# The first piece of x is issued from ScalarE's DMA queue instead of SyncE's

## The chip, the cores and the metric

The kernel runs on one core of a Trainium2 chip. The metric is device time in microseconds (us), the median over several executions of the whole program. Lower is better.

## The reference, cut to what matters

One layer of a decoder with three parallel branches over 1024 prompt tokens and 32 sample tokens (1056 rows in all, model width 1024):

```
h    = rmsnorm(x) * norm_g
proj = h @ w_in                       # (1056, 1024) x (1024, 4608)
qa, ka, va, ga, xb, gb, qc, kc, vc, gc = split(proj)
oa = rmsnorm(retention(qa, ka, va))   # branch A, 4 heads
ob = rglru(conv4(xb))                 # branch B, width 512
oc = window_attention(qc, kc, vc)     # branch C, window 128, 4 heads, 2 kv heads
y  = x + concat(oa*silu(ga), ob*silu(gb), oc*silu(gc)) @ w_out
```

All data are float32. The outputs are y for both token groups and the new states and caches. The change touches only how the first part of x reaches the chip's memory; nothing of the computation differs.

## The kernel before, in words

Each engine's instructions are written out by hand, one program per engine, and the programs meet at semaphores. There is no scheduler: the order in the file is the order on the engine.

The input projection is cut into 18 weight units of 256 columns. Every product is made in three passes of float32r matmuls (`three_pass`, L408 to L410): operands are split into a high part and a low part. The high part of a weight piece is a ScalarE copy (`w_hi`, L826), its low part a VectorE subtraction (`w_low`, L1180). For x, ScalarE multiplies with the norm gain and rounds (`x_hi`, L832), and VectorE makes the rest (`x_lo`, L1185). The row norm itself is applied later, to the projections.

At the start nothing is in memory. x comes transposed (`x_T`) in three column chunks of 352 tokens, each in four pieces of two k-blocks; the first weight unit comes in four pieces of two k-blocks too (`FIRST_PIECES`). A weight piece is 128 rows of 512 floats, an x piece 128 rows of 704 floats. The norm gains are in a small table `par`, 128 rows of 50 floats. All these transfers are issued by SyncE (SP) in one row, in the loop that starts at L272: weight piece 0 (L274), `par` (L276), x piece 0 (L277), weight piece 1, x piece 1, and so on; then the eight pieces of the other two x chunks (L280), then weight unit 1 (L267).

TensorE first runs 11 matmuls on a tile of ones (L425, 22 entries in the trace). Then `first_unit` goes through chunk 0 of x k-block by k-block. For each k-block it waits for both parts of x, and at the first of each piece for both parts of the weights, then makes six matmuls (two halves of the unit, three passes each), so twelve for a piece. Chunks 1 and 2 follow, and then units 1 to 17.

ScalarE's program begins with a table load and a one-column activation, at L1122. Then it waits for `par`, and for each piece p it waits for the weight piece, copies it, waits for the x piece and does two `x_hi`. VectorE follows it step by step.

Of the kernel before, what the change touches and what calls it, by code (L numbers as in the profile page):

```python
# [56 lines left out]
FIRST_PIECES = ((0, 2), (2, 4), (4, 6), (6, 8))  # L57
# [45 lines left out]
def layer(nc, io):  # L103
    gammas = [float(1.0 - 2.0 ** (-5.0 - h)) for h in range(H)]
    with ExitStack() as ctx:
# [3 lines left out]
        def sem(name):  # L109
            return ctx.enter_context(nc.semaphore(name))  # L110
# [37 lines left out]
        xs = [flat[:, c * KD * CH:(c + 1) * KD * CH].rearrange("p (k n) -> p k n", k=KD) for c in range(3)]  # L148
# [81 lines left out]
        S_ = {n: sem(n) for n in names}  # L230
# [23 lines left out]
        def x_part(c, k0, k1):  # L254
            return io["x_T"][c][:, k0 * CH:k1 * CH].rearrange("p (k n) -> p k n", k=k1 - k0)

        @block.sync
        def _(sp):
# [13 lines left out]
            for p, (k0, k1) in enumerate(FIRST_PIECES):  # L272
                cols = slice(k0 * UNIT, k1 * UNIT)
                sp.dma_start(raw[:, cols], io["w_units"][0][:, cols]).then_inc(S_[f"w0_in{p}"], 16)  # L274
                if p == 0:
                    sp.dma_start(par[:], io["params"]).then_inc(S_["par_in"], 16)  # L276
                sp.dma_start(xs[0][:, k0:k1, :], x_part(0, k0, k1)).then_inc(S_[f"x_in{p}"], 16)  # L277
            for c in range(1, 3):
                for q in range(4):
                    sp.dma_start(xs[c][:, 2 * q:2 * q + 2, :], x_part(c, 2 * q, 2 * q + 2)).then_inc(  # L280
# [124 lines left out]
        def _(pe):  # L405
# [16 lines left out]
            def first_unit():  # L422
                pe.wait_ge(S_["ones_set"], 1)
                for _ in range(WARM):
                    pe.matmul(bb[1][:, 0:P], ones[:], ones[:], start=True, stop=True)  # L425

                for c in range(3):
                    banks = [proj_bank(2 * c), proj_bank(2 * c + 1)]
                    cols = slice(c * CH, (c + 1) * CH)
                    if c == 2:  # L430
                        pe.wait_ge(S_["act_freed"], 2)
                    for k in range(KD):
                        pe.wait_ge(S_["h_hi_set"], KD * c + k + 1)
                        pe.wait_ge(S_["h_lo_set"], KD * c + k + 1)
                        for p, (k0, _) in enumerate(FIRST_PIECES):
                            if c == 0 and k == k0:
                                pe.wait_ge(S_["w_hi_set"], p + 1)
                                pe.wait_ge(S_["w_lo_set"], p + 1)
                        for mt in range(2):
                            w = [w_part(0, i)[:, k * UNIT + mt * P:k * UNIT + (mt + 1) * P] for i in range(2)]  # L440
                            mm = three_pass(banks[mt][:, 0:CH], w[0], w[1], h_hi[:, k, cols], h_lo[:, k, cols],
                                            k == 0, k == KD - 1)
                            if k == KD - 1:
                                mm.then_inc(S_["proj_done"], 1)
# [371 lines left out]
        def _(act):  # L816
# [11 lines left out]
            def x_hi(c, k):  # L828
                for p, (k0, _) in enumerate(FIRST_PIECES if c == 0 else ((0, 2), (2, 4), (4, 6), (6, 8))):
                    if k == k0:  # L830
                        act.wait_ge(S_[f"x_in{4 * c + p}"], 16)
                act.activation(h_hi[:, k, c * CH:(c + 1) * CH], xs[c][:, k, :], ACT.Copy,  # L832
                               scale=par[:, PAR["norm_g"] + k:PAR["norm_g"] + k + 1]).then_inc(S_["h_hi_set"], 1)
# [280 lines left out]
            def lam_exp():  # L1114
# [3 lines left out]
                act.wait_ge(S_["chain_a"], 1)  # L1118
                act.activation(sp_t[:, 1, :], sp_t[:, 0, :], ACT.Exp, scale=-1.0).then_inc(S_["lam_exp"], 1)

            act.wait_ge(S_["ones_set"], 1)
            act.activation(junk[:, 0:1], ones[:, 0:1], ACT.Copy)  # L1122
            act.wait_ge(S_["par_in"], 16)
# [690 lines left out]
```

## Time and profile before

| what | us |
|---|---|
| median of 3 runs | 708.91 |
| lowest and highest of them | 708.69, 709.2 |
| the profiled execution, its own time | 708.93 |
| its span, first to last instruction | 707.1 |
| TensorE busy in the span | 696.9 |
| ScalarE, VectorE busy in the span | 270.3, 317.3 |

The span is shorter than the time by 1.8 us, which lies outside the first and last instruction. TensorE's matmuls are pipelined: one with 352 columns is shown as 0.32 us long but one starts every 0.16 us, so gaps are read from starts.

### The profile page before, as it was taken

The numbers are of one execution on the slowest core, as the hardware profiler recorded it, in microseconds if no ns is written. First come the engines' busy times: TensorE is split into PE (matmuls) and PEld (weight loads), VectorE is DVE, ScalarE is ACT, GpSimd is POOL, SyncE is SP. The second block draws the span as 40 slices with busy tenths as digits, with TensorE's granted clock in tenths as the row PEclk, the third lists the DMA queues.
The fourth block names the chain that finished last, engine by engine and source line by source line (L and its number), as shares of the span: only waits on it lengthen the run. The fifth ranks groups of instructions, "written<-read, shape, count | busy, mean of one in ns | idle before, by whom it ended". The sixth has DMA issues, their size and how long they took to land.

```text
span 707.1 us, 11441 instructions
## 1 busy us (share of the span) xinstructions
PE 696.9 (99%) x4464; PEld 648.1 (92%) x4464; DVE 317.3 (45%) x748; ACT 270.3 (38%) x678; POOL 102.2 (14%) x215
## 2 busy tenths in 40 slices
PE   8999999999999999999999998999999999999998
PEld 8999999999999999999999998899899988888884
DVE  6462452343334539873722584328643653111113
ACT  7553233323232353558444554435542541000000
POOL 0002160535353000000012211222100000000000
PEclk9999999999999999999999999999999999999999
DMA  8402105112121301101122011211001552211111
GB/s 310 169 6 86 59 2 200 40 64 60 64 61 64 99 22 59 61 1 60 32 83 72 4 61 31 75 41 60 9 22 61 179 179 86 81 73 59 60 37 38
DMA packets 24081, 50.04 MB, mean 71 GB/s; under 512 B 1752, under 2 KB 15576, under 8 KB 21820
## 3 DMA queue, kind: packets, MB, share of 16 engines
q1 hardware_dynamic: 24028, 49.31, 20.4%
q8 instruction: 36, 0.59, 0.4%
q14 instruction: 17, 0.14, 0.1%
HBM read 42.22 MB, written 9.12 MB: 73 GB/s over the span
## 4 chain that ended last, share of the span: by engine, by line
PE 96%; DVE 2%; ACT 1%; issue 1%; DMA 1%; POOL 0%; SPq 0%; ACTq 0%
PE proj L408 21%; PE proj L410 20%; PE proj L409 20%; PE branch L410 5%; PE branch L409 5%; PE branch L408 5%; PE branch L588 2%; PE branch L653 2%; PE branch L630 1%; PE branch L504 1%; PE branch L521 1%; PE branch L536 1%; PE branch L542 1%; PE branch L524 1%; PE branch L643 1%; PE proj L786 1%
## 5 line engine op out<-in xcount | busy, mean ns | idle before, releaser
L408 PE MATMUL proj<-big 128*128 128x352 f32 (+1 forms) x952 | 305.5, 321 | 1.3 <-DVE big L1185 1.3
L409 PE MATMUL proj<-big 128*128 128x352 f32 (+1 forms) x952 | 290.6, 305 | 0.0
L410 PE MATMUL proj<-big 128*128 128x352 f32 (+1 forms) x952 | 290.4, 305 | 0.0
L408 PEld LDWEIGHTS proj<-big 128*128 128x128 f32 x952 | 179.3, 188 | 4.9 <-issue 1.9
L409 PEld LDWEIGHTS proj<-big 128*128 128x128 f32 x952 | 179.3, 188 | 2.6 <-issue 1.9
L410 PEld LDWEIGHTS proj<-big 128*128 128x128 f32 x952 | 179.2, 188 | 0.0
L1180 DVE TENSOR_TENSOR big<-raw,big 128x512 fp32r<-128x512 f32 x72 | 48.8, 689 | 37.9 <-ACT big L826 37.7
L1646 POOL TENSOR_SCALAR stat<-stat 128x1 f32<-128x1 f32 (+2 forms) x68 | 17.9, 264 | 292.4 <-ACT junk L952 191.0
L410 PE MATMUL branch<-big,m_parts 128*128 128x512 f32 x144 | 56.0, 389 | 0.0
L409 PE MATMUL branch<-big,m_parts 128*128 128x512 f32 x144 | 56.0, 389 | 0.0
L408 PE MATMUL branch<-big,m_parts 128*128 128x512 f32 x144 | 56.0, 389 | 0.0
L1445 DVE TENSOR_TENSOR m_parts<-mixed,m_parts 128x1024 fp32r<-128x1024 f32 (+3 forms) x18 | 15.2, 887 | 76.4 <-ACT m_parts L1111 76.4
L1111 ACT ACTIVATE m_parts<-mixed 128x1024 fp32r<-128x1024 f32 (+3 forms) x18 | 13.4, 784 | 86.0 <-PE branch L410 56.4
L826 ACT ACTIVATE big<-raw 128x512 fp32r<-128x512 f32 x72 | 44.1, 626 | 2.4 <-DMA par<-params 2.0
L1647 POOL TENSOR_TENSOR stat<-stat 128x1 f32<-128x1 f32 (+2 forms) x68 | 40.1, 589 | 5.7
L1278 DVE SCALAR_TENSOR_TENSOR sT<-branch,stat,cr 128x128 f32<-128x128 f32 (+1 forms) x36 | 12.2, 338 | 58.2 <-PE branch L504 54.2
L409 PEld LDWEIGHTS branch<-big,m_parts 128*128 128x128 f32 x144 | 27.0, 188 | 5.6
L408 PEld LDWEIGHTS branch<-big,m_parts 128*128 128x128 f32 x144 | 27.0, 188 | 5.6
L410 PEld LDWEIGHTS branch<-big,m_parts 128*128 128x128 f32 x144 | 27.0, 188 | 5.5
L1416 DVE SCALAR_TENSOR_TENSOR kn<-proj,stat,gain 128x128 f32<-128x128 f32 (+1 forms) x18 | 6.3, 350 | 49.9 <-POOL stat L1647 49.9
L905 ACT ACTIVATE o_nrm<-branch,stat 128x128 f32<-128x128 f32 x32 | 11.8, 367 | 41.7 <-DVE mixed L1319 33.4
L891 ACT ACTIVATE mixed<-proj 128x352 f32<-128x352 f32 x24 | 11.0, 461 | 38.4 <-PE proj L410 38.4
(239 smaller groups left out, 982.8 us busy)
## 6 DMA issues: line engine op xcount, KB each, us to landing
raw<-w_units SPq DMA_DIRECT2D x17, 1024.0 KB, 4.9
mixed<-x_T SPq DMA_DIRECT2D x12, 352.0 KB, 7.4
x_res<-x_prompt SPq DMA_DIRECT2D x8, 512.0 KB, 4.2
out_y_prompt<-y_out SPq DMA_DIRECT2D x8, 512.0 KB, 2.9
raw<-w_out SPq DMA_DIRECT2D x6, 512.0 KB, 3.9
y_out<-w_out SPq DMA_DIRECT2D x6, 512.0 KB, 4.5
s<-state_ret SPq DMA_DIRECT2D x4, 512.0 KB, 4.0
out_s_ret<-s SPq DMA_DIRECT2D x4, 512.0 KB, 3.2
```

The lines of the kernel that those rows point to most:

```text
L408: pe.matmul(out, a_lo, b_hi, start=first, stop=False)
L409: pe.matmul(out, a_hi, b_lo, start=False, stop=False)
L410: return pe.matmul(out, a_hi, b_hi, start=False, stop=last)
L588: pe.matmul(bb[GATE_BANKS[q]][:, 0:CH], wg[:, gate, f, :], cv[:, f % 2, c * CH:(c + 1) * CH], start=True, stop=True).then_inc(S_["gates_do ...
L653: mm = pe.matmul(bb[3][:, 0:2 * P], v_c[:, half, t - 1 + kt, :], pT[:, n8 % 2, kt * 2 * P:(kt + 1) * 2 * P], start=(kt == 0 or t == 0), st ...
L826: act.activation(w_part(u % 2, 0)[:, cols], raw[:, cols], ACT.Copy).then_inc(S_["w_hi_set"], 1)
L1111: act.activation(hi, mixed[:, rows, chunk_cols(t)], ACT.Copy).then_inc(S_["m_hi_set"], 1)
L1180: dve.tensor_tensor(w_part(u % 2, 1)[:, cols], raw[:, cols], w_part(u % 2, 0)[:, cols].bitcast(F32), ALU.subtract).then_inc(S_["w_lo_set"], 1)
L1278: dve.scalar_tensor_tensor(out=sT[0:n, m % 2, 0:n], in0=bb[0][0:n, 0:n], scalar=rcol[0:n, c:c + 1], in1=mask, op0=ALU.mult, op1=ALU.mult). ...
L1445: dve.tensor_tensor(lo, mixed[:, rows, chunk_cols(t)], hi.bitcast(F32), ALU.subtract).then_inc(S_["m_lo_set"], 1)
L1646: link(pool.tensor_scalar(ss, ss, 1.0 / DH, ecol[0:n, t:t + 1], ALU.mult, ALU.add))
L1647: return pool.tensor_tensor(rs, ss, neghalf[0:n, 0:w], ALU.pow)
```

## The change

The transfer of x piece 0 leaves SP's list, where it stood third. ScalarE issues the same transfer, from the same source to the same place and with the same semaphore, as its first instruction.

```
@@ SyncE's first loop
                 if p == 0:
                     sp.dma_start(par[:], io["params"]).then_inc(S_["par_in"], 16)
-                sp.dma_start(xs[0][:, k0:k1, :], x_part(0, k0, k1)).then_inc(S_[f"x_in{p}"], 16)
+                if p > 0:
+                    sp.dma_start(xs[0][:, k0:k1, :], x_part(0, k0, k1)).then_inc(S_[f"x_in{p}"], 16)
@@ the start of ScalarE's program
+            act.dma_start(xs[0][:, 0:FIRST_PIECES[0][1], :], x_part(0, *FIRST_PIECES[0])).then_inc(S_["x_in0"], 16)
             act.wait_ge(S_["ones_set"], 1)
             act.activation(junk[:, 0:1], ones[:, 0:1], ACT.Copy)
             act.wait_ge(S_["par_in"], 16)
```

On SP, the first instructions before the change; `raw` is a weight piece, `mixed` the place where x lands:

```order
L274 DMA raw<-w_units 128x512
L276 DMA par<-params 128x50
L277 DMA mixed<-x_T 128x704
L274 DMA raw<-w_units 128x512
L277 DMA mixed<-x_T 128x704
```

and after it:

```order
L274 DMA raw<-w_units 128x512
L276 DMA par<-params 128x50
L274 DMA raw<-w_units 128x512
L278 DMA mixed<-x_T 128x704
L274 DMA raw<-w_units 128x512
```

The first x piece is gone from SP's third place, and all that stood behind it has moved up by one.

On ScalarE, the first instructions before the change (`big` holds the split parts):

```order
L1122 ACT_TABLE_LOAD
L1122 ACTIVATE junk<-ones 128x1
L826 ACTIVATE big<-raw 128x512
L832 ACTIVATE big<-mixed,par 128x352 x2
L826 ACTIVATE big<-raw 128x512
```

and after it:

```order
L1122 DMA mixed<-x_T 128x704
L1124 ACT_TABLE_LOAD
L1124 ACTIVATE junk<-ones 128x1
L827 ACTIVATE big<-raw 128x512
L833 ACTIVATE big<-mixed,par 128x352 x2
```

The transfer's issue now stands ahead of the table load; the rest of ScalarE's program is in the same order.

## Rows read from the trace of the kernel before

**Rows 1.** The page, part 1 (busy us) and part 4 (the chain by engine).

```profile
PE 696.9 (99%) x4464; PEld 648.1 (92%) x4464; DVE 317.3 (45%) x748; ACT 270.3 (38%) x678; POOL 102.2 (14%) x215
PE 96%; DVE 2%; ACT 1%; issue 1%; DMA 1%; POOL 0%; SPq 0%; ACTq 0%
```

**Rows 2.** Waits of TensorE, whole span: total us, times, longest.

```profile
PE branch L667 <- ACT kcT L1010: 1.8, 2, 0.9
PE branch L643 <- ACT pT L1006: 1.4, 2, 0.9
PE proj L408 <- DVE big L1185: 1.3, 1, 1.3
PE branch L425 <- POOL ones L1682: 1.1, 1, 1.1
PE branch L699 <- DVE kcT L1507: 0.9, 1, 0.9
PE branch L563 <- DVE mixed L1319: 0.3, 1, 0.3
```

**Rows 3.** Chain of work, 0 to 7.6 us: start us, us, what.

```profile
0.73 0.38 SPq L274
...
1.17 0.42 SPq L276
...
1.63 4.23 DMA mixed<-x_T
...
5.88 0.60 ACT big L832
...
6.50 0.60 DVE big L1185
...
7.19 0.40 PE proj L408
```

**Rows 4.** ScalarE in order of time, first 17 us.

```profile
0.73 1.28 ACT L1122 ACT_TABLE_LOAD   x1 [0.73 <-PEq L1806]
2.03 0.20 ACT L1122 ACTIVATE junk<-ones 128x1 f32<-128x1 f32 x1
4.26 0.63 ACT L826 ACTIVATE big<-raw 128x512 fp32r<-128x512 f32 x1 [2.03 <-DMA par<-params]
5.88 1.07 ACT L832 ACTIVATE big<-mixed,par 128x352 fp32r<-128x352 f32 x2 [0.99 <-DMA mixed<-x_T]
6.86 0.61 ACT L826 ACTIVATE big<-raw 128x512 fp32r<-128x512 f32 x1
7.84 1.07 ACT L832 ACTIVATE big<-mixed,par 128x352 fp32r<-128x352 f32 x2 [0.37 <-DMA mixed<-x_T]
9.11 0.63 ACT L826 ACTIVATE big<-raw 128x512 fp32r<-128x512 f32 x1 [0.20 <-DMA raw<-w_units]
9.98 1.07 ACT L832 ACTIVATE big<-mixed,par 128x352 fp32r<-128x352 f32 x2 [0.24 <-DMA mixed<-x_T]
...
11.55 4.91 ACT L832 ACTIVATE big<-mixed,par 128x352 fp32r<-128x352 f32 x10
```

**Rows 5.** TensorE in order of time: the warm-up, and the restart at 11.29.

```profile
1.15 4.78 PE L425 MATMUL branch<-ones 128*128 128x128 f32 x22 [1.15 <-POOL ones L1682]
...
10.97 0.32 PE L410 MATMUL proj<-big 128*128 128x352 f32 x1
11.29 0.40 PE L408 MATMUL proj<-big 128*128 128x352 f32 x1
11.53 0.32 PE L409 MATMUL proj<-big 128*128 128x352 f32 x1
```

**Rows 6.** TensorE's first unit behind the restart, last: PE clock, DMA share, GB/s.

```profile
11.29:30.50 19.21, 19.21 (x121) 19.21 (x121) 12.53 (x24) 12.96 (x28) 0.00 (x0) 1.00 0.76 292
```

**Rows 7.** SP's issues in order: start us, us, line [idle before].

```profile
1.63 0.43 SPq L277 DMA_DIRECT2D mixed<-x_T  x1
2.11 0.43 SPq L274 DMA_DIRECT2D raw<-w_units  x1
2.58 0.43 SPq L277 DMA_DIRECT2D mixed<-x_T  x1
3.53 0.43 SPq L277 DMA_DIRECT2D mixed<-x_T  x1
```

**Rows 8.** Issue to landing (last number, us): weights 0, par, x 0, x 1, x 2.

```profile
raw<-w_units SPq DMA_DIRECT2D x1, 256.0 KB, 3.1
par<-params SPq DMA_DIRECT2D x1, 25.0 KB, 3.1
mixed<-x_T SPq DMA_DIRECT2D x1, 352.0 KB, 4.2
mixed<-x_T SPq DMA_DIRECT2D x1, 352.0 KB, 5.2
mixed<-x_T SPq DMA_DIRECT2D x1, 352.0 KB, 6.4
```

**Rows 9.** Stretches of the start, same columns as rows 6.

```profile
1.70:2.30 0.60, 0.60 (x5) 0.60 (x4) 0.00 (x0) 0.52 (x2) 0.00 (x0) 1.00 0.69 171
2.30:2.80 0.50, 0.50 (x4) 0.50 (x3) 0.00 (x0) 0.00 (x0) 0.00 (x0) 1.00 0.80 280
2.80:3.60 0.80, 0.80 (x5) 0.80 (x5) 0.00 (x0) 0.00 (x0) 0.00 (x0) 1.00 0.68 118
3.60:10.00 6.40, 5.13 (x30) 4.92 (x29) 3.69 (x7) 3.94 (x8) 0.00 (x0) 1.00 0.98 309
```

**Rows 10.** VectorE in order of time, around 12 us.

```profile
12.22 5.04 DVE L1185 SCALAR_TENSOR_TENSOR big<-mixed,par,big 128x352 fp32r<-128x352 f32 x10
```

More of the change, by code:

```diff
@@ L276, in _ @@
                     sp.dma_start(par[:], io["params"]).then_inc(S_["par_in"], 16)
-                sp.dma_start(xs[0][:, k0:k1, :], x_part(0, k0, k1)).then_inc(S_[f"x_in{p}"], 16)
+                if p > 0:
+                    sp.dma_start(xs[0][:, k0:k1, :], x_part(0, k0, k1)).then_inc(S_[f"x_in{p}"], 16)
             for c in range(1, 3):
@@ L1119, in lam_exp @@
                 act.activation(sp_t[:, 1, :], sp_t[:, 0, :], ACT.Exp, scale=-1.0).then_inc(S_["lam_exp"], 1)
+            act.dma_start(xs[0][:, 0:FIRST_PIECES[0][1], :], x_part(0, *FIRST_PIECES[0])).then_inc(S_["x_in0"], 16)
             act.wait_ge(S_["ones_set"], 1)
```

## The prediction

> **What bounds the kernel now.** The busy times and the shares of the chain come first [rows 1]: TensorE is busy 696.9 of 707.1 us, and 96% of the chain that ends last is TensorE. No other engine is busy half of the span. The kernel can only get shorter by what TensorE waits, or by cheaper matmuls, and this change touches no matmul. So the next view is that of TensorE's waits [rows 2]. They sum to 5.8 us. Five of the six are within the work of a branch, or at the very first instruction (the memset of the ones), and move along with TensorE. One has to do with the change: 1.3 us, once, until VectorE has made the first low part of x.
>
> The chain of the first 7.6 us tells what stands behind that wait [rows 3]. SP issues weights 0 at 0.73 and par at 1.17, x 0 is issued at 1.63 and lands 4.23 us later, at 5.86; ScalarE's first x_hi takes 0.60 us, VectorE's x_lo 0.60, and the first projection matmul starts at 7.19. ScalarE had idled 0.99 us for x 0, having been done with its weight copy at 4.26 + 0.63 = 4.89 [rows 4]. So x 0 is late by a microsecond against what stands beside it.
>
> The next thing to see is that x 0 is not the only late piece. ScalarE waits for x 1 until 7.84, and for x 2 until 9.98 [rows 4]. TensorE starts a matmul every 0.16 us, but the one after 10.97 starts at 11.29 instead of 11.13 and the next one follows after 0.24 [rows 5]: the restart costs 0.16 + 0.08 = 0.24 us. It waits there for x 2, which had landed 1.31 us before (11.29 - 9.98). From 11.29 to 30.5 TensorE is busy without a gap [rows 6]. Whatever the start gives back thus has to come through two gates: the first matmul (7.19), and the arrival of x 2 (its matmul at 11.29). Behind the second gate everything hangs on TensorE, and shifts as it shifts.
>
> **The change part by part.**
>
> *On SP.* One issue less. The step from one issue to the next is 2.11 - 1.63 = 0.48 us [rows 7], so weights 1, x 1 and all behind them are issued about 0.47 us earlier. That alone means little: x 1 is issued at 2.58 and takes 5.2 us to land, x 2 is issued at 3.53 and takes 6.4 [rows 7, 8]. Each further piece takes longer than the one before, so they stand in a queue of bytes, not of issues. Weights 0 and par keep their issue times (0.73 and 1.17).
>
> *On ScalarE.* One issue more, ahead of the table load. Priced as one on SP, 0.43 us [rows 7]. It moves the table load and the one-column activation from 0.73..2.23 to about 1.2..2.7. ScalarE then waits for par until 4.26 [rows 4], so the cover is 2.03 us and the cost nothing. Without that cover it would be 0.43 us on the path. GpSimd, VectorE and TensorE start as before; the ones come from GpSimd, so the warm-up matmuls (1.15 to 5.93 [rows 5]) don't move. They set a floor: no projection matmul starts before 5.93, 1.26 us ahead of today's 7.19.
>
> *x 0 itself* is issued at 0.73 instead of 1.63, 0.90 us earlier. How much earlier it lands is what the trace doesn't show, as no second queue runs there. The lower bound of the gain is nothing, the upper bound 0.90 us, if the bytes were not in each other's way. They are. I work it out in bytes. Weights 0, par and x 0 are 256 + 25 + 352 KB = 648 thousand bytes [rows 8]. In the stretches [rows 9] the DMA engines moved 0.6 x 171 = 103 thousand bytes until 2.3, 0.5 x 280 = 140 until 2.8, and 0.8 x 118 = 94 until 3.6, 337 in all; then they run at 309 GB/s. The missing 311 thousand take 1.01 us: all three are moved at 4.61. The landing at 5.86 is 1.25 us later; that is what the slowest engine and the notice of completion add.
>
> The stretch from 2.8 to 3.6 at 118 GB/s is the hole which the change can fill. Weights 0 are nearly through there, par's short rows trickle, and x 0, issued 0.9 us behind weights 0, is only coming in. With x 0 queued from the start I take the full 309 GB/s from 2.3 on: 103 thousand bytes by 2.3, then 545 / 309 = 1.76 us, so all three are moved at 4.06, 0.55 us earlier than 4.61. **The whole front of bytes moves by 0.55 us**, x 1 and x 2 with it. Between the ends for this (0 if the hole is par's own doing, 0.55 + 0.6 x (309 - 171) / 309 = 0.82 if two queues fill the ramp too) I take 0.55, since the rate of 280 just ahead of the hole is near 309 already.
>
> *The first gate.* x 0 then lands at 5.86 - 0.55 = 5.31 at the latest. But ScalarE does the weight copy first, and it needs par, which stands behind weights 0 in SP's queue, while x 0 now moves beside them. Before, weights 0 and par (288 thousand bytes) were moved at 2.8 + 45 / 118 = 3.18, and par landed at 4.26 (1.17 + 3.1), 1.08 later. At one end par keeps its time; then x 0 decides and the gate moves by 0.55. At the other end the two queues share evenly, par is moved last of the three, at 4.06, and lands at 4.06 + 1.08 = 5.14; the copy lasts until 5.77, and x_hi starts at 5.77 instead of 5.88: the gate moves by 0.11.
>
> The Trainium skill bears on this (DMA: Bandwidth & Descriptors, "Queues, rings and completion order" and "Issuing engines are not separate DMA queues"): the queues of SP and ACT run on the same 16 engines, each engine takes turns between queues packet by packet, and a second issuer saves only the sequencer's time. No row here shows two queues at once. By it the gate would move by the 0.11, not the 0.55.
>
> *The sum.* The time gained is the smaller of two: what the first gate gives plus the restart that goes away (0.11 to 0.55, plus 0.24), and what the second gate gives (0.55). That is 0.35 to 0.55 us. I take 0.4. What would be late next is the last piece: ScalarE begins its x_hi at 11.55 [rows 4], VectorE's x_lo at 12.22 is one of ten in 5.04 us and done by 12.8 [rows 10], and TensorE wants it twelve matmuls behind 11.29, at 13.3. That is 0.5 us of slack, and this chain moves with the front too. From 708.93 us, the time of the profiled execution (the median, 708.91, is the same to 0.02), this is **708.5 us**. A measurement of this kernel can tell about 0.2%, or 1.4 us, from no change; by that bound this is no change.
>
> **The rivals.**
>
> 1. *The transfers don't disturb each other.* x 0 lands 0.90 earlier, par as before, and two queues fill the ramp as well. The first gate gives 0.90 (6.29, above the floor of 5.93), the second 0.82: the smaller of 0.90 + 0.24 and 0.82. It gives 708.1. For it: only 171 GB/s in the ramp. Against it: 309 GB/s is held for 6.4 us at a DMA share of 0.98, so the engines are full there.
>
> 2. *Slower: par and weights 0 pay for x 0.* If the hole belongs to par's rows of 200 bytes (DMA share is 0.68 in it while it moves 118 GB/s), the front doesn't move, and all three pieces land together at 5.86. Then ScalarE starts the weight copy at 5.86, ends it at 6.49, and x_hi starts 0.61 later than now. The first matmul starts at 7.80; 0.24 is given back as the restart goes. The loss is 0.37 us: 709.3. It decides at par's landing: past 4.26 + 0.99 = 5.25 the first matmul is later than before, past 5.49 the kernel is slower.
>
> 3. *It does not do what it says.* ScalarE's issue lands its data no earlier than SP's third did (both issuers share one generator of transfers, or ScalarE's first instruction begins late). ScalarE's table load starts at 0.73 as SP's first issue does [rows 3, 4], which speaks against the late start. The time is 708.9.
>
> **How the numbers follow.** The forecast (gain of 0.2 to 0.6) has 0.58, rival 1 (0.6 to 1.1) has 0.10, rival 2 (a loss of 0.1 to 0.6) 0.15, rival 3 and what is near zero 0.14; 0.03 are left for something that moves over 1.4 us, such as a handshake far behind that falls differently when everything shifts. The three runs of before spread over 0.5 us, so I widen the ends of 708.1 and 709.3 a little: 707.9 to 709.4. No case above reaches 0.2%: same has 0.97, faster and slower share the rest.
>
> **What would show it right or wrong.** In the changed kernel's chain, the first matmul starts between 6.6 and 7.1, and the restart near 11.29 is gone, with TensorE running at 0.16 us a start from its first projection matmul to 30 us. The stretch from 2.8 to 3.6 us shows about 300 GB/s instead of 118. par lands at about 5.1 instead of 4.26, and ScalarE's idle time ahead of the first x_hi has gone from 0.99 to near nothing, with the wait ahead of the weight copy grown by as much. ScalarE's wait for x 2 ends at about 9.4. The prediction is wrong if par lands beyond 5.5, if that stretch keeps its hole, or if the last matmul of the span doesn't move by what the first unit's does.

## The result and the profile after

The changed kernel takes 710.64 us as the median of 22 executions, the kernel before 709.10 us as the median of 22 beside them. The ratio is 1.0016, with a 95% interval of 1.0009 to 1.0023: slower by 1.5 us between the medians and 1.2 us between the means (710.32 and 709.16). That is within the 0.2% that I called no change, but it is a clear move, to the side that I did not forecast. The profiled execution took 710.37 us, its span is 708.6 us against 707.1.

The single times tell more than the median. Eight of the 22 lie between 708.71 and 709.56 us, fourteen between 710.37 and 712.61. Of the kernel before, twenty lie below 709.5 and two at 710.34 and 710.57. So there are two groups, and the change moves executions from one into the other. The means of the changed kernel's groups are 708.96 and 711.10, 2.1 us apart; the twenty of the kernel before have a mean of 709.03. The record also has the mean granted clock of every execution: of the fourteen late ones of the changed kernel thirteen have 0.995 to 0.998 and one (712.35) has 1.000; all eight early ones have 0.999 or 1.000.

The chain of work of the changed kernel, 0 to 14 us (start us, us, what), answers to [rows 3]:

```profile
0.73 0.38 SPq L274
...
1.17 4.08 DMA par<-params
...
5.27 0.64 ACT big L827
...
6.00 0.69 DVE big L1182
6.70 0.51 DVE big L1187
...
7.29 0.40 PE proj L409
...
7.85 0.23 PE proj L411
8.09 0.29 PE proj L409
```

The chain no longer runs through x piece 0 but through par, which lands at 5.25 us instead of 4.26. Behind it stand the weight copy on ScalarE, the low part of the weights on VectorE (0.69), and only then x_lo. The first projection matmul starts at 7.29, 0.10 later than before. Then something happens which the kernel before does not show: from the fourth matmul on, one starts every 0.29 us instead of every 0.16.

ScalarE in order of time, the changed kernel, beside [rows 4]:

```profile
0.73 0.40 ACTq L1122 DMA_DIRECT2D mixed<-x_T  x1
1.16 1.28 ACT L1124 ACT_TABLE_LOAD   x1 [1.16 <-PEq L1808]
2.46 0.20 ACT L1124 ACTIVATE junk<-ones 128x1 f32<-128x1 f32 x1
5.27 0.63 ACT L827 ACTIVATE big<-raw 128x512 fp32r<-128x512 f32 x1 [2.61 <-DMA par<-params]
5.80 1.05 ACT L833 ACTIVATE big<-mixed,par 128x352 fp32r<-128x352 f32 x2
6.76 0.61 ACT L827 ACTIVATE big<-raw 128x512 fp32r<-128x512 f32 x1
7.45 1.07 ACT L833 ACTIVATE big<-mixed,par 128x352 fp32r<-128x352 f32 x2
8.43 0.61 ACT L827 ACTIVATE big<-raw 128x512 fp32r<-128x512 f32 x1
8.95 1.07 ACT L833 ACTIVATE big<-mixed,par 128x352 fp32r<-128x352 f32 x2
```

The wait for x 0 is gone and the wait for par has grown. x 1 and x 2 are no longer waited for: ScalarE begins them at 7.45 and 8.95 instead of 7.84 and 9.98. The data came earlier, as meant.

Stretches of the changed kernel; the last three numbers are TensorE's granted clock, the DMA share and GB/s. The first four rows answer to [rows 9], the rest cuts the time behind the first matmul:

```profile
1.70:2.30 0.60, 0.60 (x5) 0.60 (x4) 0.00 (x0) 0.60 (x1) 0.00 (x0) 1.00 0.80 151
2.30:2.80 0.50, 0.50 (x4) 0.50 (x3) 0.00 (x0) 0.35 (x2) 0.00 (x0) 1.00 0.66 126
2.80:3.60 0.80, 0.80 (x5) 0.80 (x5) 0.00 (x0) 0.00 (x0) 0.00 (x0) 1.00 0.98 327
3.60:10.00 6.40, 4.50 (x24) 4.34 (x23) 4.00 (x8) 4.65 (x10) 0.00 (x0) 0.83 1.01 365
...
7.29:7.90 0.61, 0.60 (x4) 0.61 (x5) 0.61 (x2) 0.53 (x2) 0.00 (x0) 0.91 0.95 355
7.90:11.20 3.30, 3.30 (x13) 3.30 (x13) 3.30 (x7) 3.24 (x8) 0.00 (x0) 0.50 1.03 399
11.20:30.50 19.30, 19.30 (x123) 19.30 (x122) 11.70 (x23) 12.08 (x25) 0.00 (x0) 1.00 0.71 270
```

The hole from 2.8 to 3.6 is filled (327 GB/s instead of 118), though the stretch ahead of it fell from 280 to 126. In bytes, 0.6 x 151 + 0.5 x 126 + 0.8 x 327 = 415 thousand are moved by 3.6, where the kernel before had 337: 78 thousand more, or 0.25 us at 309 GB/s. Behind 3.6 the rate is 365 GB/s, where it was 309. And from 7.9 to 11.2 the granted clock is 0.50, that is 1.2 GHz instead of 2.4. TensorE's own waits, which answer to [rows 2], and the end of its warm-up, which answers to the first of [rows 5]:

```profile
PE proj L409 <- DVE big L1187: 1.9, 1, 1.9
...
1.15 4.25 PE L426 MATMUL branch<-ones 128*128 128x128 f32 x22 [1.15 <-POOL ones L1684]
7.29 0.40 PE L409 MATMUL proj<-big 128*128 128x352 f32 x1 [1.90 <-DVE big L1187]
```

The other five waits are the same to 0.1 us. The whole difference between the two traces lies in the first 12 us: 12 matmuls at 0.29 instead of 0.16 us are 1.56 us, the first matmul is 0.10 later, the restart of 0.24 is gone; 1.56 + 0.10 - 0.24 = 1.42, where the spans differ by 1.5. The idle stretch ahead of the first matmul is 1.90 us instead of 1.27, but of these 0.63 us only 0.10 are the later start: the other 0.53 come from the warm-up, which ended at 5.40 in this execution and at 5.93 in that of the kernel before, with the same matmuls. So this pair of traces alone does not show that the change made the stretch longer.

### The profile page after: what moved, and what is told of

The parts are those of the page before. It is cut to its first block, busy times and chain, and to the rows that moved or that the text cites. A ratio compares the mean times of both kernels' runs of the same rounds, so it can differ in the third digit from the quotient of the medians.

```text
span 708.6 us, 11441 instructions
## 1 busy us (share of the span) xinstructions
PE 697.7 (98%) x4464; PEld 649.2 (92%) x4464; DVE 316.9 (45%) x748; ACT 270.3 (38%) x678; POOL 102.2 (14%) x215
## 4 chain that ended last, share of the span: by engine, by line
PE 96%; DVE 2%; ACT 1%; issue 1%; DMA 1%; POOL 0%; SPq 0%; ACTq 0%; DVEq 0%
PE proj L409 21%; PE proj L411 21%; PE proj L410 21%; PE branch L411 5%; PE branch L409 5%; PE branch L410 5%; PE branch L589 2%; PE branch L654 2%; PE branch L631 1%; PE branch L505 1%; PE branch L522 1%; PE branch L537 1%; PE branch L543 1%; PE branch L525 1%; PE branch L644 1%; PE proj L787 1%
```

## The experiments

**Theory.** The loss has two parts. The larger is TensorE's clock: TensorE idles between the warm-up and the first projection matmul, and in more executions than before its clock is at 1.2 GHz for 3.3 us after it. The smaller is par, which now lands later since it stands behind weights 0, while these share the engines with x 0. **Rivals:** the clock falls because of what the transfers do, whatever TensorE did; and a second queue in itself costs the time.

### More warm-up on the changed kernel, less and more on the kernel before

On the changed kernel:

```
-        WARM = 11
+        WARM = 15
```

> The changed kernel with 15 instead of 11 warm-up matmuls on the tile of ones. Theory (gap): the change costs time because TensorE sits idle between the end of the warm-up (5.39 in the changed kernel's trace) and the first projection matmul (7.29), 1.90 us instead of 1.27, and the granted clock falls to the lower level for about 3.4 us soon after in most executions, at 12 matmuls x 0.13 us = 1.5 us each time. Four more warm-ups at some 0.2 to 0.4 us fill most of the gap: the clock stays at 1.00, and the time is 708.3 to 708.8, below the kernel before. Rival (data): the clock falls because of what the DMA engines or the data do then, whatever TensorE did before: 710.6 as the changed kernel. Rival (chain): the time was lost further back in the program: 710.6 too, with clock at 1.00.

Measured: 709.59 us, 709.02 to 709.88 in 11 executions; ratio 1.0005 (0.9996 to 1.0013). The group above 710 is gone, as the theory said, though no transfer was touched and the first matmul of the trace below starts later than in the changed kernel's. That speaks against the rival of the transfers: the same transfers, with more warm-up, lose the clock in none of 11 executions. But the time is above the kernel before, not below: the expected 708.3 to 708.8 is missed by 0.8. TensorE in the profiled execution:

```profile
1.14 5.26 PE L426 MATMUL branch<-ones 128*128 128x128 f32 x30 [1.14 <-POOL ones L1684]
...
7.98 0.40 PE L409 MATMUL proj<-big 128*128 128x352 f32 x1 [1.58 <-DVE big L1187]
8.22 0.32 PE L410 MATMUL proj<-big 128*128 128x352 f32 x1
8.38 0.32 PE L411 MATMUL proj<-big 128*128 128x352 f32 x1
...
2.50:4.50 2.00, 2.00 (x11) 2.00 (x10) 0.00 (x0) 0.16 (x1) 0.00 (x0) 1.00 0.93 261
4.70:6.30 1.60, 1.60 (x16) 1.51 (x14) 0.00 (x0) 0.34 (x1) 0.00 (x0) 1.00 1.02 354
```

The matmuls are at full pace from the first (0.16 us from start to start), but the first starts at 7.98: ScalarE waited for par until 5.96 here. The last two rows show the warm-up itself: 11 of its entries touch the 2.00 us of the first, 16 the 1.60 us of the second. One starts every 0.21 us until 4.6, then every 0.11: the pace doubles. Both rows read 1.00. The 1.00 of the early rows is thus no sign of full pace.

The kernel before with the same edit:

> The kernel before with 15 warm-up matmuls. Theory (gap): its gap of 1.27 us rarely makes the clock fall (two of its 22 executions were over 710.3), so filling it brings the median nothing but removes such outliers: 708.9 to 709.2, none above 709.6. If the fifteen last beyond 7.19, each 0.1 us beyond costs 0.1 us. Rival (data): same times with outliers as before.

Measured: 709.18 us, 708.69 to 709.63; ratio 1.0001 (0.9992 to 1.0010). None of 11 is above 709.9, where 2 of the 33 of the kernel before beside it are. With the warm-up filled in both, the change costs 709.59 - 709.18 = 0.41 us between the medians and 0.39 between the means of 11 and 11, which is 3.4 standard errors. That is the part without the clock.

The kernel before, with its 11 warm-up matmuls cut to 8:

```
-        WARM = 11
+        WARM = 8
```

> The kernel before with 8 instead of 11 warm-up matmuls, its transfers untouched. Theory (gap): the warm-up ends 0.6 to 1.3 us earlier, the idle stretch ahead of 7.19 grows from 1.27 to about 2 or 2.5 us, and the clock falls in most executions, as in the changed kernel: 710.5 to 711. Rival (data): no transfer has moved, so no change: 709.1.

Measured: 710.07 us, 709.07 to 711.55; ratio 1.0013 (1.0005 to 1.0022). Eight of 11 are above 709.9, and no transfer was touched; the expected 710.5 to 711 is missed by 0.4. So TensorE's program alone can lose 1 us. But the way there is another one than in the changed kernel: of the eight, seven have a mean granted clock of 1.000 and one has 0.997. The profiled execution:

```profile
7.28 0.63 PE L408 MATMUL proj<-big 128*128 128x352 f32 x1 [2.35 <-DVE big L1185]
7.71 0.50 PE L409 MATMUL proj<-big 128*128 128x352 f32 x1
...
7.28:10.70 3.42, 3.42 (x12) 3.42 (x13) 3.15 (x6) 3.04 (x7) 0.00 (x0) 1.00 1.02 362
10.70:14.00 3.30, 3.30 (x22) 3.30 (x21) 3.30 (x8) 3.29 (x8) 0.00 (x0) 1.00 1.05 417
```

12 matmuls are in the 3.42 us from 7.28, 22 in the 3.30 after: the pace is that of 1.2 GHz until 10.7. The slow pace is there from the first matmul on, whereas the changed kernel's first three ran at full pace. The warm-up of 16 entries in 3.78 us had not come to full pace when it ended: one started every 0.21 us to the last. The granted clock in the row is 1.00 all the same, as it is over the slow half of the warm-up above. So there are two ways to slow matmuls: the clock comes up in the warm-up and falls after the idle stretch, and the row reads 0.50; or it has not come up yet, and the row reads 1.00. The pace of the matmuls has to be read too, since the granted clock alone misses the second.

### The changed kernel once more

> The changed kernel itself once more, for a second trace of it. Theory (gap): its executions fall in two groups, 708.7 to 709.6 with TensorE at full pace from its first projection matmul, and 710.4 or more with some 12 matmuls at 0.29 us a start. The landing of par, and so the first matmul, varies between executions from about 7.3 to 8.0. Rival: every execution has the slow matmuls and the spread comes from elsewhere.

Measured: 710.57 us; four executions at 709.38 to 709.82, six at 710.44 to 712.17. Both groups are there again. ScalarE waits for par until 6.07, the first matmul starts at 8.09:

```profile
6.07 0.63 ACT L827 ACTIVATE big<-raw 128x512 fp32r<-128x512 f32 x1 [3.40 <-DMA par<-params]
...
8.10:9.70 1.60, 1.60 (x10) 1.60 (x11) 1.60 (x4) 1.60 (x5) 0.00 (x0) 0.96 1.01 357
9.70:12.90 3.20, 3.20 (x13) 3.20 (x12) 3.20 (x7) 3.20 (x7) 0.00 (x0) 0.50 1.04 413
```

The warm-up ended at 6.22 in this execution, the idle stretch was 1.88 us, and the clock fell at 9.6, nine matmuls after the restart. In three traces with x 0 on ScalarE's queue and par behind weights 0, ScalarE begins its first copy at 5.27, 5.96 and 6.07; in the three with the transfers of the kernel before, at 4.26, 4.02 (8 warm-ups) and 4.65 (15). The two sets don't overlap. Beside the changed kernel's first trace, this one starts its first matmul 0.80 us later and takes 0.78 longer (711.15 against 710.37), with the clock lost in both. So a late start comes on top of the 1.5 us of the clock, which is how the two groups can lie 2.1 us apart.

### The order and the queue of par

par from ScalarE too, ahead of x 0 (SP's issue of par is taken out):

```
+            act.dma_start(par[:], io["params"]).then_inc(S_["par_in"], 16)
             act.dma_start(xs[0][:, 0:FIRST_PIECES[0][1], :], x_part(0, *FIRST_PIECES[0])).then_inc(S_["x_in0"], 16)
```

> The changed kernel with par issued from ScalarE too, ahead of x piece 0. Theory (par behind weights 0 in SP's queue, while x 0 takes turns with them, made par land at 5.25 instead of 4.26): par lands near 3.5, weights 0 or x 0 decide instead, the first projection matmul starts at 6.4 to 6.9, the idle stretch shrinks to some 1.2 us, the clock falls seldom: 708.2 to 708.8. Rival (all transfers that are in flight land together at about 5.2 whatever their order): first matmul at 7.2 to 7.3 and 710.6.

Measured: 711.24 us, 709.77 to 712.49; ratio 1.0024 (1.0015 to 1.0033), worse than the change. The theory's numbers are missed altogether. The landings, issue to landing in the last number, of weights 0, par and x 0, and the clock:

```profile
raw<-w_units SPq DMA_DIRECT2D x1, 256.0 KB, 4.0
par<-params ACTq DMA_DIRECT2D x1, 25.0 KB, 4.1
mixed<-x_T ACTq DMA_DIRECT2D x1, 352.0 KB, 5.6
...
8.08:14.20 6.12, 6.12 (x21) 6.12 (x22) 6.12 (x13) 6.12 (x14) 0.00 (x0) 0.50 1.04 403
```

par has a tenth of the bytes of weights 0, and was issued at the same time on a queue of its own; it lands 0.1 us after them, at 4.8. Both have 128 rows. And x 0, now second on its queue and issued at 1.17, lands at 6.77, with weights 1 of SP's queue at 6.5. That fits queues which take turns row by row: what starts together ends together, however short the rows of one are. The packets of each queue tell it directly. Between 3 and 4 us of the changed kernel's trace, with weights on SP's queue (q1) and x 0 on ScalarE's (q10):

```profile
q10 hardware_dynamic: 70, 0.20, 59.6%
q1 hardware_dynamic: 66, 0.13, 40.0%
```

The second number is MB. 70 packets against 66 are nearly equal turns, at 0.20 against 0.13 MB: the packets are rows of 2816 and of 2048 bytes. With par on q10, from 2.5 to 3.5 us of this run, the counts are 72 and 63, at 0.01 and 0.11 MB. The Trainium skill says in DMA: Bandwidth & Descriptors, "Queues, rings and completion order", that each engine takes turns between the queues packet by packet, and the traces agree with it here; that a packet is one row is what these traces show.

The time follows from the late x 0: the first matmul starts at 8.08, after 2.88 us of idle. The clock had fallen before the matmuls began, and the row has it at 0.50 for 6.1 us. Of the 11 executions seven have a mean granted clock of 0.995 to 0.998.

par ahead of weights 0 on SP, x 0 alone on ScalarE's queue:

```
+                if p == 0:
+                    sp.dma_start(par[:], io["params"]).then_inc(S_["par_in"], 16)
                 sp.dma_start(raw[:, cols], io["w_units"][0][:, cols]).then_inc(S_[f"w0_in{p}"], 16)
-                if p == 0:
-                    sp.dma_start(par[:], io["params"]).then_inc(S_["par_in"], 16)
```

> The changed kernel with par ahead of weights 0 in SP's list; x piece 0 stays ScalarE's first instruction. Theory (turns row by row: two transfers that start together end together whatever their row size, since each has 8 rows per DMA engine; in the changed kernel weights 0 and x 0 ended together and par behind them): now par pairs with x 0, both land near 4.0 to 4.3, weights 0 follow and land last, at 5.0 to 5.4. The weight copy waits for them, the first projection matmul starts at 7.1 to 7.4 as in the changed kernel, and the time is 710 to 711. Rival (shares by bytes, small par costs nothing): par lands near 3, weights 0 and x 0 together near 4.9, the first matmul starts at 6.8 and the time is 708.6 to 709.5.

Measured: 708.58 us, 708.42 to 710.24, one of 11 above 709.9; ratio 0.9990 (0.9981 to 0.9999). Swapping two issues turns the change from a loss into a small gain. Landings of x 0, par and weights 0, then ScalarE and TensorE:

```profile
mixed<-x_T ACTq DMA_DIRECT2D x1, 352.0 KB, 3.2
par<-params SPq DMA_DIRECT2D x1, 25.0 KB, 2.7
raw<-w_units SPq DMA_DIRECT2D x1, 256.0 KB, 3.6
...
4.82 0.63 ACT L827 ACTIVATE big<-raw 128x512 fp32r<-128x512 f32 x1 [2.15 <-DMA raw<-w_units]
...
6.85 0.40 PE L409 MATMUL proj<-big 128*128 128x352 f32 x1 [0.93 <-DVE big L1187]
```

par pairs with x 0 (3.43 and 3.93), and weights 0 come last (1.17 + 3.6 = 4.77): the order that I expected, but all three land earlier than I had put them, x 0 by 0.1 and par by 0.6 us at least, the first matmul starts at 6.85 instead of 7.1 or later, and the time is that of the rival. The order of the landings fits turns by rows, but par and x 0 are 0.5 us apart, and from 1.7 to 2.8 us the trace has 132 packets on par's queue against 64 on x 0's: at the very start the turns are not equal. How long the landings take I had wrong.

The same order with x 0 still third on SP:

> The kernel before with par ahead of weights 0 on SP, x piece 0 still third on SP. It tells whether par first alone brings the gain or only together with x 0 on ScalarE's queue. Theory (x 0's landing is what the first matmul waits for in the kernel before, and it stays third of three in one queue): par lands near 3.5, weights 0 near 4.4, x 0 near 5.8; the first matmul at 7.0 to 7.2; 709.0 to 709.3, as before. Rival (par's short rows made the hole, and as the first transfer they hide in the ramp): x 0 lands near 5.3, first matmul at 6.7, 708.6.

Measured: 709.26 us, ratio 0.9998 (0.9989 to 1.0007), first matmul at 7.17: no gain. The profiled execution, 710.23 us, is one of the three above 710; its first 12 matmuls are slow, as with 8 warm-ups:

```profile
1.15 5.06 PE L425 MATMUL branch<-ones 128*128 128x128 f32 x22 [1.15 <-POOL ones L1682]
7.17 0.63 PE L408 MATMUL proj<-big 128*128 128x352 f32 x1 [0.97 <-DVE big L1185]
```

So par first is worth something only together with x 0 on the other queue, as far as two sessions can be laid side by side, each against its own runs of the kernel before; the second queue in itself does not cost, it pays once the short table is out of its way.

par, and not x 0, on ScalarE's queue:

> The kernel before with par, not x piece 0, moved to ScalarE as its first instruction; x 0 moves up to second place on SP. Theory (turns row by row): par ends together with weights 0, near 4.4, and x 0, issued at 1.17, fills the hole in the bytes between 2.8 and 3.6 us: it lands near 5.4, the first projection matmul starts at 6.6 to 6.9, the gap behind the warm-up is under 1.2 us, the clock seldom falls: 708.4 to 708.9, none of the large x transfer sharing its turns with anything. Rival (a second queue in itself costs what the change cost): first matmul at 7.3 or later, 709.6 to 711.

Measured: 708.75 us, 708.14 to 709.28; ratio 0.9988 (0.9979 to 0.9997). None of 11 is above 709.3, where ten of the 27 of the kernel before beside it are above 709.9. par and weights 0 land together again (4.4 and 4.3 from their issues at 0.73), but x 0 lands at 5.97, not 5.4, and the first matmul of the profiled execution starts at 7.28. The time came out as expected, the way there only in part: the first matmul is no earlier than before (7.19), and a part of the gain is that no execution is in the late group. The idle stretch of its trace is 1.72 us, and the clock held:

```profile
7.28 0.40 PE L406 MATMUL proj<-big 128*128 128x352 f32 x1 [1.72 <-DVE big L1184]
```

That was longer than the expected 1.2, and it falls in with the other traces, as the next part tells.

par first and 14 warm-up matmuls:

> The changed kernel with par ahead of weights 0 on SP and 14 instead of 11 warm-up matmuls. Theory: the first projection matmul starts at about 6.85 as with par first alone, the warm-up now ends at 6.2 to 6.9, and no execution shows slow matmuls: 708.4 to 708.7, none above 709.5. Rival (the warm-up had nothing to do with the few slow executions left): one or two in eleven still above 709.5.

Measured: 708.72 us, 708.34 to 709.99; ratio 0.9990 (0.9981 to 0.9999). Ten of 11 are below 708.9; that none would be above 709.5 is missed by one. The eleventh is the profiled one, and its matmuls are at full pace throughout; it is late since weights 0 landed at 6.4 and the first matmul started at 8.46:

```profile
6.43 0.63 ACT L827 ACTIVATE big<-raw 128x512 fp32r<-128x512 f32 x1 [3.77 <-DMA raw<-w_units]
...
8.46 0.40 PE L409 MATMUL proj<-big 128*128 128x352 f32 x1 [1.50 <-DVE big L1187]
```

So the one outlier is not the clock's, and an uneven landing of the first pieces is a second source of spread. Beside par first alone (708.58 in another session, with the same ratio of 0.9990), the longer warm-up brings nothing that can be measured.

## Why the prediction was wrong

*Right:* the bound (TensorE, with nothing moved behind the first 12 us); the cover of ScalarE's issue (table load until 2.44, par at 5.25); the hole of 2.8 to 3.6, filled to 327 GB/s; par's landing at 5.25, where I had 5.14 for even sharing; the restart near 11.29, gone. The second gate opened as meant, and nothing came through it.

*Right in direction, not in size: the front of bytes.* I moved it by 0.55 us as a whole. By 3.6 us it had moved by 0.25; ScalarE begins x 1 at 7.45 instead of 7.84, 0.4 earlier, and x 2 at 8.95 instead of 9.98, 1.0 earlier. The later part comes from the 365 GB/s behind 3.6, for which I had kept 309 (the three traces with the transfers of the kernel before have 304 to 320 there). That TensorE's waits sum to 5.8 us was a slip, the six rows make 6.8; nothing hung on it.

*A term mis-sized: the first gate.* I had 0.11 to 0.55 earlier, and it was 0.10 later in the profiled execution, and 0.8 to 0.9 in two other traces (7.98, 8.09). In the first, the copy starts at 5.27, 0.13 later than I had it, and still x_hi starts at 5.80 against 5.88 before. What makes the gate late is a step that I left out: VectorE makes the low part of the weights (0.69 us) ahead of x_lo. Before, it was done by 5.69, well ahead of x_hi's end; now it starts at 6.00, and x_lo behind it at 6.70 instead of 6.50. The other two traces show par landing up to 0.8 us later still, which my single sum of bytes could not tell. The rival in which par and weights 0 pay for x 0 was right in that: weights 0 land at 4.83 instead of 3.83 (0.73 + 4.1, 0.73 + 3.1), par at 5.25 instead of 4.26. It was wrong in its premise that the front stays where it is, and in the landing at 5.86 for all three; x 0 is down by 5.03. That its 0.37 us is near the 0.41 measured with the warm-up filled is therefore in part luck. I gave it 0.15.

*The step that failed: each matmul priced at 0.16 us.* I used the warm-up only as a floor, "no projection matmul starts before 5.93", and took the full pace behind it as given. The runs show 0.29 us for 12 of them, at a granted clock of 0.50. The full pace is what the warm-up buys, and the data have to come in time for it to last. 14 of 22 executions are in the late group, where 2 of 22 were before; the trace of one shows 1.5 us for the clock. In means: 0.39 (both kernels with 15 warm-ups) + (14 - 2) / 22 x 1.5 = 0.82 gives 1.2 us; the means of the 22 and 22 are 1.16 apart. The two parts account for the loss, as an estimate: the 0.39 is from another session, and the 1.5 from one trace.

*Open:* what decides in which execution the clock falls. Nine traces have their warm-up's clock up before the first projection matmul. In six of them it held, with idle stretches of 0 (the kernel before with 15 warm-ups), 0.93, 1.27, 1.50, 1.58 and 1.72 us; in three it fell, with 1.88, 1.90 and 2.88. The order is without exception, but the traces are few, of different kernels, and no run varies the stretch alone, so I take no limit from them. The other way to slow matmuls does not depend on the stretch: in the trace of the kernel before with par first it was 0.97 us, and the 22 entries of the warm-up had started 0.21 us apart to the last, 5.06 us in all. Both ways occur in the kernel before: of its ten late executions in one session four have a mean granted clock of 0.997 or 0.998, six 0.999 or 1.000. The same kernel also varies between sessions: 2 of 33, 10 of 27 and 5 of 21 executions of the kernel before were above 709.9. The Trainium skill (TensorE: Matmul & The Clock Gate, "What's actually happening") says that where the clock rises varies from run to run; the warm-ups of 22 entries in these traces took from 4.06 to 5.07 us, which agrees.

## What to carry to other kernels

When a first piece of data is moved to a second queue, it does not jump the line. It takes turns with what the first queue holds, here row by row, so ask which small transfer stands behind the large one that it now shares with: here a table of 25 KB that everything waits for had to go first. And where a kernel warms TensorE up ahead of its first data, the pace behind the warm-up is no given: here first data that came later by 0.4 us in the mean went with the clock lost in 14 of 22 executions instead of 2, at 1.5 us each. Look at the spread of single times, at each one's mean granted clock and at the pace of the first matmuls before calling such a change neutral.

## What the runs showed of the hardware

- Two transfers of 128 rows that start together on SP's and ScalarE's queues can land together, though a row is 200 bytes in one and 2048 in the other: 4.8 and 4.7 us for par (25 KB) and weights (256 KB) in one kernel, 5.1 and 5.0 in another. While both queues hold data, the packets come nearly one for one (70 and 66 between 3 and 4 us of the changed kernel). With rows of 200 and 2816 bytes and the short ones on SP's queue, the landings were 0.5 us apart (3.43 and 3.93).
- An idle stretch of 1.90 us, behind a warm-up of 4.25 us, was followed by 3.3 us at a granted clock of 0.50 (1.2 GHz). The fall came 0.5 us after matmuls had started again in one trace, 1.5 us after in another, and still within the idle stretch of 2.88 us in a third.
- The granted clock in the rows reads 1.00 over stretches in which the matmuls show the pace of 1.2 GHz: over the slow part of the warm-up (a start every 0.21 us until 4.6 us, 0.11 after, in the changed kernel with 15 warm-ups), and from 7.28 to 10.7 us in the kernel before with 8 warm-ups (0.29 us a start for 352 columns).
